# Third layer, sparse attention: both heads of a pair turned through one PSUM bank, one after the other

## What is computed

```python
g = sigmoid(gates)
merged = g[:, :, 0] * o_a + g[:, :, 1] * o_b + g[:, :, 2] * o_m
```

## Time and profile before

| | |
|---|---|
| median of 3 runs | 2210.07 us (2203.17 to 2214.13) |
| the profiled execution | 2206.05 us |
| its span, first to last instruction | 2204.2 us |
| TensorE busy | 2117.1 us, 96% |
| VectorE busy | 967.0 us, 44% |
| ScalarE busy | 866.5 us, 39% |
| GpSimd busy | 840.0 us, 38% |
| mean granted TensorE clock | 0.989 |
| waits of TensorE from 1600 to 1760 us | 15.0 us |

### The profile page before, as it was taken

The page is one execution under the profiler, slowest core; times in us unless marked ns, Lnnn a source line. Parts: engine busy times, 40 slices in busy tenths (PEclk is TensorE's granted clock), DMA queues, the critical chain, the costliest instruction groups (busy, mean ns, idle before and its releaser), DMA issues. The chain is left out here.

```text
span 2204.2 us, 26734 instructions
## 1 busy us (share of the span) xinstructions
PE 2117.1 (96%) x10366; PEld 1684.7 (76%) x10366; DVE 967.0 (44%) x1642; ACT 866.5 (39%) x1769; POOL 840.0 (38%) x447
## 2 busy tenths in 40 slices
PE   8999999999899999989999999999999899999998
PEld 6788888887658767678778888787774478888886
DVE  2444645444444575654571311258666532111211
ACT  4554556564344565543331232333322232221221
POOL 4433233332333323353444445344333152444442
PEclk9999999999999999999999999999999999999999
DMA  6313233232622212132433333233344242323321
GB/s 220 96 58 96 58 96 97 77 97 78 222 92 73 88 58 77 51 122 77 134 96 107 90 101 105 83 93 99 104 149 130 85 153 67 96 96 96 96 96 58
DMA packets 130204, 218.67 MB, mean 99 GB/s; under 512 B 8712, under 2 KB 58552, under 8 KB 129872
## 3 DMA queue, kind: packets, MB, share of 16 engines
q1 hardware_dynamic: 111152, 169.68, 25.3%
q0 software_dynamic: 8096, 28.93, 4.1%
q10 hardware_dynamic: 10832, 18.35, 2.4%
HBM read 198.29 MB, written 18.04 MB: 98 GB/s over the span
## 5 line engine op out<-in xcount | busy, mean ns | idle before, releaser
L2530 POOL TENSOR_TENSOR lo_ring<-raw_ring,hi_ring 128x1024 fp32r<-128x1024 f32 (+1 forms) x288 | 694.5, 2434 | 1009.2 <-ACT hi_ring L2173 1009.1
L1117 PE MATMUL bank<-xh,hi_ring 128*128 128x512 f32 (+1 forms) x1568 | 610.7, 389 | 3.6 <-DVE xl L1601 2.9
L1117 PE MATMUL bank<-xh,lo_ring 128*128 128x512 f32 (+1 forms) x1568 | 593.9, 379 | 0.0
L1117 PE MATMUL bank<-xl,hi_ring 128*128 128x512 f32 (+1 forms) x1568 | 592.6, 378 | 0.0
L2173 ACT CAST hi_ring<-raw_ring 128x1024 fp32r<-128x1024 f32 (+1 forms) x288 | 288.1, 1045 | 406.5 <-PE bank L1117 385.3
L1117 PEld LDWEIGHTS bank<-xh,hi_ring 128*128 128x128 f32 x1568 | 297.1, 189 | 66.2 <-issue 13.8
L1117 PEld LDWEIGHTS bank<-xh,lo_ring 128*128 128x128 f32 x1568 | 296.5, 189 | 56.4
L1117 PEld LDWEIGHTS bank<-xl,hi_ring 128*128 128x128 f32 x1568 | 297.2, 190 | 52.7 <-issue 2.2
L1117 PE MATMUL bank<-hi_ring,xh 128*128 128x512 f32 (+1 forms) x512 | 209.4, 409 | 9.7 <-DVE xl L1755 4.9
L1117 PE MATMUL bank<-hi_ring,xl 128*128 128x512 f32 (+1 forms) x512 | 201.5, 394 | 0.0
L1117 PE MATMUL bank<-lo_ring,xh 128*128 128x512 f32 (+1 forms) x512 | 201.2, 393 | 0.0
(11 more groups left out here) (289 smaller groups left out, 2675.2 us busy)
## 6 DMA issues: line engine op xcount, KB each, us to landing
raw_ring<-in_ffn_w_in SPq DMA_DIRECT2D x176, 256.0 KB, 3.1
raw_ring<-in_dil_w_in SPq DMA_DIRECT2D x80, 512.0 KB, 3.6
raw_ring<-in_ffn_w_out SPq DMA_DIRECT2D x44, 512.0 KB, 3.7
raw_ring<-in_diff_w_in SPq DMA_DIRECT2D x32, 512.0 KB, 3.7
raw_ring<-in_w_in SPq DMA_DIRECT2D x32, 512.0 KB, 3.6
arena<-scratch_heads POOLq DMA_DIRECT2D x4, 1584.0 KB, 12.0
scratch_gates<-arena ACTq DMA_DIRECT2D x24, 256.0 KB, 2.0
arena<-scratch_gates POOLq DMA_DIRECT2D x24, 256.0 KB, 5.0
```

The lines of the kernel that those rows point to most:

```text
L1117: ins = T.matmul(bank[pb][:, cols if p.form == "feature" else slice(0, p.cols)], lhsT, rhs, start=(k == 0 and m == 0 and half != 1), stop= ...
L2530: G.tensor_tensor(lo, raw_ring[:, p % RAW, 0:q.kq * q.n], hi.bitcast(F32), ALU.subtract).then_inc(lowered, 1)
```

## The change

The second slot of a round turns head 0 only, into bank 7. Head 1 is turned in the third slot, into bank 7 as well, ahead of values n - 2. ScalarE copies head 0, VectorE head 1, as before. The half microsecond of room ahead of a turn back is gone, and the turn back is issued behind the third slot's room, right ahead of the next round's scores. The second `ss_turn` goes to bank 5 instead of bank 4. The waits that named the old banks and job numbers name the new ones.

```diff
@@ sparse_heads
             if 1 <= n <= N:
-                plan.job("s_turn", *jobs[n - 1], banks=(7, 6))
+                plan.job("s_turn", *jobs[n - 1], 0, banks=(7,))
             yield wait
+            if 1 <= n <= N:
+                plan.job("s_turn", *jobs[n - 1], 1, banks=(7,))
             if n >= 2:
                 b, j = jobs[n - 2]
                 plan.job("s_values", b, j, banks=(4,) if j == 0 else ())
-                if j == 3:
-                    yield 0.5
-                    plan.job("s_back", b, banks=(5,))
             yield wait
+            if n >= 2 and j == 3:
+                plan.job("s_back", b, banks=(5,))
@@ state_begin
         for r in range(2):
-            plan.job("ss_turn", r, banks=(4,))
+            plan.job("ss_turn", r, banks=(4 + r,))
             yield 1.0
@@ TensorE
-            def s_turn(job, b, j):
-                T.wait_ge(s_exped, job.n + 1)
-                for c in range(2):
-                    tb = 7 - c
-                    empty(tb, job.use[c])
-                    for k in range(b + 1):
-                        ins = T.transpose(tile(bank[tb], k), tile(h_work[job.n % 2][:, c, :], k), ident)
-                    ins.then_inc(filled[tb], 1)
+            def s_turn(job, b, j, c):
+                T.wait_ge(s_exped, 4 * b + j + 1)
+                empty(7, job.use[0])
+                for k in range(b + 1):
+                    ins = T.transpose(tile(bank[7], k), tile(h_work[j % 2][:, c, :], k), ident)
+                ins.then_inc(filled[7], 1)
 
             def s_values(job, b, j):
-                for c in range(2):
-                    T.wait_ge(drained[7 - c], use_of["s_turn", job.n][c])
+                T.wait_ge(drained[7], use_of["s_turn", 2 * job.n + 1][0])
...
             def ss_in(job, comp):
                 if comp == 0:
-                    T.wait_ge(drained[4], use_of["ss_turn", 1][0])
+                    T.wait_ge(drained[4], use_of["ss_turn", 0][0])
+                    T.wait_ge(drained[5], use_of["ss_turn", 1][0])
@@ VectorE
-                elif kind == "s_turn":
-                    nk = (a[0] + 1) * P
-                    V.wait_ge(filled[6], job.use[1])
-                    V.tensor_copy(h_pt[:, job.n % 2, 1, 0:nk], bank[6][:, 0:nk]).then_inc(drained[6], 1)
+                elif kind == "s_turn" and a[2]:
+                    b, j, c = a
+                    nk = (b + 1) * P
+                    V.wait_ge(filled[7], job.use[0])
+                    V.tensor_copy(h_pt[:, j % 2, c, 0:nk], bank[7][:, 0:nk]).then_inc(drained[7], 1)
@@ ScalarE
-                elif kind == "s_turn":
-                    nk = (a[0] + 1) * P
-                    copy_out(7, job.use[0], h_pt[:, job.n % 2, 0, 0:nk], bank[7][:, 0:nk])
+                elif kind == "s_turn" and not a[2]:
+                    b, j, c = a
+                    nk = (b + 1) * P
+                    copy_out(7, job.use[0], h_pt[:, j % 2, c, 0:nk], bank[7][:, 0:nk])
@@ GpSimd
                     if a[0] == "ffn2":
-                        G.wait_ge(filled[6], use_of["s_turn", 15][1])
+                        G.wait_ge(filled[7], use_of["s_turn", 31][0])
```

More of the change, by code:

```diff
@@ L1365, in ss_turn @@
                 T.wait_ge(u_ordered, 2 * r + 2)
-                empty(4, job.use[0])
+                empty(4 + r, job.use[0])
                 for i in range(8):
                     g = 8 * r + i
-                    ins = T.transpose(bank[4][:, i * NCH:(i + 1) * NCH], u_by_group[:, g * P:(g + 1) * P], const("ident", NCH)[:, 0:NCH])
-                ins.then_inc(filled[4], 1)
+                    ins = T.transpose(bank[4 + r][:, i * NCH:(i + 1) * NCH], u_by_group[:, g * P:(g + 1) * P], const("ident", NCH)[:, 0:NCH])
+                ins.then_inc(filled[4 + r], 1)
             def ss_in(job, comp):
                 if comp == 0:
-                    T.wait_ge(drained[4], use_of["ss_turn", 1][0])
+                    T.wait_ge(drained[4], use_of["ss_turn", 0][0])
+                    T.wait_ge(drained[5], use_of["ss_turn", 1][0])
                 empty(4, job.use[0])
@@ L1951, in s_score @@
                 if job.n >= 2:
-                    V.wait_ge(filled[6], use_of["s_turn", job.n - 2][1])
+                    V.wait_ge(filled[7], use_of["s_turn", 2 * (job.n - 2) + 1][0])
                 else:
@@ L2114, in vector_program @@
                         V.wait_ge(drained[3], keep_use["q"][3])
-                        V.wait_ge(filled[4], use_of["ss_turn", 1][0])
+                        V.wait_ge(filled[5], use_of["ss_turn", 1][0])
                     q_means.append(head_means(by_head(proj_q[:, 2 * i:2 * i + 2, :].rearrange("p n c -> p (n c)")), norm_stat[:, 48 * i:48 * i + 16],
@@ L2494, in scalar_program @@
                 elif kind == "ss_turn":
-                    copy_out(4, job.use[0], U[:, 8 * a[0]:8 * a[0] + 8, :], bank[4][:, :].rearrange("p (a b) -> p a b", a=8))
+                    copy_out(4 + a[0], job.use[0], U[:, 8 * a[0]:8 * a[0] + 8, :], bank[4 + a[0]][:, :].rearrange("p (a b) -> p a b", a=8))
                 elif kind == "ss_in":
```

## The result

| | changed kernel | before, same comparison | ratio, 95% interval |
|---|---|---|---|
| first comparison | 2220.6 us (6 runs, 2217.6 to 2224.4) | 2209.8 us | 1.0051 (1.0033 to 1.0070) |
| second comparison | 2225.2 us (6 runs, 2218.1 to 2230.6) | 2207.8 us | 1.0081 (1.0062 to 1.0099) |

The change made the kernel slower by some 11 us in the first comparison and 17 in the second, clear of noise in both. For the second, 2218 to 2222 had been expected, so it came out 3 us above that. The first profiled execution took 2217.6 us, with a span of 2215.8, 11.6 us more than before. Lines have moved: scores are L1335 now, the turns L1341, values L1351, the turn back L1359, the state input's turns L1367, the main products L1118. The exponentials stay L2350 and the copies L2287.

A forecast was written before the change was run, and what follows sets the result against it. TensorE, busy 96% of the span, was taken to bound the kernel by its work plus idle time. Terms -2.7 - 7.2 + 23.6 - 1.6 - 3.0 + 0.7 + 1.6 = +11.4, say +11, on 2208.4 gave 2219.5 us, range 2207 to 2232.

The forecast's parts named there:

- State input, -2.7: At the state input's second turn, TensorE's wait for ScalarE's copy of bank 4 goes whole: -2.7 us.
- Lost waits, -7.2: At the pairs' turns, six waits on bank 6 (6.2 us) and one on ScalarE (1.0) go: -7.2 us.
- New waits, 23.6: The second head's turn waits for ScalarE's copy of the first out of bank 7, behind exponentials: +23.6 us.
- the 3 us of arrears: At scores 11 to 13 TensorE's earlier waits let late VectorE catch up: 3 of 6.7 us taken back.
- Turn backs, -1.6: At turn back 2 TensorE arrives later and waits less for VectorE's L1976: -1.6 us together with VectorE's reordering.
- Score after turn back 2, +0.7: With no slot or main product between turn back 2 and the next score, a new wait there: +0.7 us.
- Idle time in all: TensorE's idle time in the stage grows by 12.5 us.
- Clock, +1.6: New TensorE idles over 2 us bring one 4 us stretch of lowered clock: +1.6 us, bounds 0 and +5.
- Score 1 to score 15: A sign to check: TensorE's time from score 1 to score 15 grows from 113.7 to about 125 us.
- the copy is prompt: Rival: ScalarE copies the first head once turned; the eight bare turns wait about 3 us; 2202 us; chance 0.10.
- The waits only move: Rival: VectorE and ScalarE set the stage's pace, so later waits are repaid: +1 us, 2209; chance 0.15.
- The clock pays too: Rival: each wait over 2 us brings 1.2 GHz, VectorE's lateness isn't made up: +19 us, 2227; chance 0.20.

The follow-up runs named there:

- the state input alone: Kernel before the change, with only the state input's second turn moved to bank 5: 2203.2 us against 2206.3, ratio 0.9990.
- the pairs alone: Changed kernel with the state input's second turn back in bank 4, as before the change: 2226.7 us, ratio 1.0089.
- ScalarE copies first: Changed kernel, with ScalarE copying the first head of turn n - 1 ahead of the exponentials of pair n: 2204.6 us, ratio 0.9990.
- the run through bank 6: Changed kernel with the second head still in its own slot but turned into bank 6: 2196.4 us, ratio 0.9946.

## Why the prediction was right, point by point

The time, 2219.5, is 1 us from the first comparison and 6 below the second, which lies inside the forecast's own range of 2212 to 2226, and the mechanism is the one forecast. Its terms fared less evenly: the idle time was put 1 to 3 us too high and the clock 3 to 5 us too low. That these two errors cancelled is luck, and so is the single microsecond.

- *State input, -2.7.* The gap is gone, and with the state input alone score 0 came 2.8 us sooner.
- *Lost waits, -7.2.* All gone: no turn waits on VectorE.
- *New waits, 23.6.* Measured by score, with the forecast in brackets: 1: 3.62 (3.6); 4: 1.50 (1.4); 6: 0.55 (1.1); 7: 1.05 (1.1); 8: 1.86 (1.9); 10: 2.28 (3.2); 11: 1.32 (2.3); 12: 1.26 (1.1); 13: 1.85 (3.3); 14: 0.82 (0.8); 15: 2.71 (2.8); turn 15: 0.77 (0.8); none at 2, 3, 5 and 9 (0.2). The sum is 19.6. The forecast less the 3 us of arrears was 20.6, and the three waits from which these were taken gave 2.3 us less. In the second comparison's profile they did wait that long, 1.32, 1.37 and 3.43, nearly the 6.7 read from the rows. Reading "copy end less score start" from the rows before works wherever the engines between are as late as they were there.
- *Turn backs, -1.6.* Measured -3.7. Turn back 2 didn't wait at all. VectorE's fold (L1586 before) had taken 2.7 us there beside POOL's mask addition, and takes 0.69 in this profile. Score 13's wait varies with the first step of a fold (L1582) in the same way. Here are the first comparison's row and then two of the second's:

```profile
1715.40 0.43 DVE L1582 TENSOR_SCALAR arena<-arena 128x512 f32<-128x512 f32 x1 [3.13 <-ACT arena L2237]
...
1718.85 2.34 POOL L2660 TENSOR_TENSOR consts<-consts,arena 128x1024 f32<-128x1024 f32 x1 [6.71 <-DMA consts<-scratch_table]
1719.47 2.00 DVE L1582 TENSOR_SCALAR arena<-arena 128x512 f32<-128x512 f32 x1 [3.13 <-ACT arena L2237]
```

  The step takes 0.43, 2.00 and, with the pairs alone, 2.56 us, and the wait is 1.85, 3.43 and 3.98 us: the same differences to 0.01 us. The long ones began after POOL's addition, the short one before it.
- *Score after turn back 2, +0.7.* Measured 2.1 for three instead of 1.4 for two.
- *Idle time in all.* The forecast was +12.5; 24.4 less 15.0 is +9.4, and +11.1 in the second profile. It was 1 to 3 us too much.
- *Clock, +1.6.* This is the term that was mis-sized. By the timed runs it is +4.8 and +6.5, at and above the upper bound of 5. The charge over the stage, +8.6 in the first profile and +3.5 in the second, can't settle it, since the state input alone, with the pairs as before, also has 10.3 instead of 6.8. I counted idles over 2 us and took one of four. What I missed, at least for the first profile, is that the last rounds have no main product left: the low clock stayed from 1743 to 1763, through 48 small products, and came back 3.4 us after the `merge` products began. No run tests this by itself. Before, it fell only at the last turn back (1745 to 1752), and in the second comparison too (1759 to 1766). Why it fell earlier in the first profile stays open.
- *Score 1 to score 15.* 1614.21 to 1736.64 is 122.4 us, and 125.9 in the second profile; the forecast said about 125, from 113.7.

Of the rivals, *the copy is prompt* describes the kernel in which ScalarE copies first: it gave 2204.6 where the rival had 2202. In the changed kernel the copy isn't prompt. The rule of the Trainium skill (PSUM — Partial Sum Buffer, summary of rules for kernel authors) that a bank being read is to be left alone points the right way, 24 us by the run through bank 6. But the read itself is 0.25 to 0.6 us; two thirds of the price, 16 us, went when the exponentials no longer stood ahead of it in ScalarE's queue, and 3.1 of the 8.4 us of waits left then stood behind the bias load and the casts. *The waits only move* is out: turning two jobs round on ScalarE took 11 us of waits or more away from the turns, and only 2.7 came back, at the turn backs. *The clock pays too* had more in it than its 0.20: its clock, 5 on top of my 1.6, is as large as measured in the second comparison, and there its arrears came as well. Its +19 stands beside +17.4 there, my +11 beside +10.8 in the first.

What stays open: how much of the loss is the 11 of the first and the 17 of the second comparison. The two profiles differ by 1.7 us of waits (19.6 and 21.3) and the runs by 1.7 us of clock, which is about half of the difference.

## What to carry to other kernels

When two steps are put through one PSUM bank, the wait between them runs, as here, to the end of everything ahead of that read in the reader's queue, with what that in turn waits for (here VectorE's maximum). So measure "end of the copy less start of the round" and not the copy. Before a bank is given up to save a wait, ask whether the steps can be moved apart with the banks kept: here the split with both banks kept was 0.5% faster (0.1% of it the state input's), and sharing the bank turned it to 0.5 to 0.8% slower. Idle time of TensorE came with a clock cost of its own: in the four comparisons that added 9 to 23 us of waits, each microsecond of it went with 0.5 to 0.8 us by the clock.

## What the runs showed of the hardware

Useless transposes made the changed kernel faster: 157 of them in twelve waits took 7 to 13 us off, with a granted clock of 1.00 instead of 0.96 from 1640 to 1720 us and 0.91 instead of 0.78 in the 40 us after. The idle time that brings the clock down has no single length in these traces: 1.5 us at turn 1 did in the kernel before, 2.72 us at the state input didn't, and a wait of 2.3 us at 1547 to 1550 in the kernel before was followed by 0.69 and in the changed kernel, with the same wait, by 1.00. The wait of 2.71 us at score 15 brought 0.50 in one profile of the changed kernel and left 1.00 in the other.

VectorE's step L1582 (0.43 us alone) took 1.93, 2.00 and 2.56 us in three profiles in which it began during POOL's mask addition (L1583 at 1707.50 in the kernel before, L1581 with the pairs alone), and ended 0.28 us after that addition each time.
